# Forget sums of cached pages moved into the projection, and three small stages made one

## The chip, the cores and the metric

The kernel is one launch on 1 core of one Trainium2 chip. The metric is the device time of that launch in microseconds (us), lower is better. TensorE (PE) multiplies matrices, VectorE (DVE) and ScalarE (ACT) do elementwise work, GpSimd (POOL) helps with both and issues gathers, SyncE (SP) issues most transfers. "DMA queue" below is the row of transfers that one of these engines has issued; all of SP's go through the profile's queue q1.

## The reference: what is computed

One layer of a decoder over a prompt of 2,048 tokens (prefill) and over 8 requests of 8 new tokens, each with 8,192 cached positions in 64 pages of 128.

```python
p = einsum('btd,de->bte', x, w_in)          # q | k | v | 8 forget logits | 512 pooling channels
logf = log_sigmoid(f_logit + b_f)
qc = cumsum(logf, axis=1)                   # forget sums of the new tokens
kc_past = lf_past - cumsum(lf_past, axis=1, reverse=True)   # of the cached positions
s = q.k * ATTN_SCALE + qc[query] - kc[key]; p = softmax(causal(s)); att = p @ v
pool[g] = window_mean(u[g], 2**(g+1)) - u[g]; pool = (pool @ w_pool) * pool_scale
x1 = layer_norm(ALPHA * x + concat(att, pool) @ w_out)
x2 = layer_norm(ALPHA * x1 + conv_ffn(x1))
```

`kc_past` of a cached position is minus the sum of the forget terms of all later cached positions of its request. `cache_logf` holds one row per page: 128 positions x 8 heads, 4 KB; `page_table` says which pages a request owns.

## The kernel before

The work is a row of stages. Each is a block of its own with one instruction stream per engine; its end waits until its transfers have landed, clears its semaphores and passes a barrier of all engines. Every matrix product in fp32 is three products of rounded parts (`hi`, `lo`).

**`stage_project`** (tiles `A_`). `w_in` comes in eight 1 MB chunks through the two halves of `prow`; ACT makes `w_hi` (L289), DVE `w_lo` (L326), and only then may SP load the next chunk into that half (`w_lo_done`). Then 17 tiles of 128 tokens with 5 column groups each. PE does a group's 24 products (L214 to L216); ACT copies out groups 0, 2, 4 and DVE groups 1 and 3 (L313). Between groups PE turns q, k and u of the tile before (L226) and the next x (L198); DVE makes the rests of both (L318, L303). POOL copies the gates and splits v. SP stores the results and loads the x of a tile ahead (L151).

**`stage_gates_pool`** (tiles `B_`). SP loads eight constants and the 4 MB `uT`. DVE makes the log-sigmoid as a chain of short instructions, `lf`; PE sums it (`ps_s`, `ps_c`); DVE scales and splits the sums into `css` and `ch`. SP stores them (`negc_s`, `aug`). Then for each of four pooling groups DVE makes window sums and `pooled` (L488 to L496), PE multiplies with `w_pool` (L530), ACT scales (L510), SP stores `poolT` (L439, L441).

**`stage_prepare`** (tiles `E_`). It readies decode attention. SP loads constants, four copies of the sample queries, the keys and `negc_s`, and copies v into groups (`vgrp`, L1116). DVE clears `qbd` and `wn`, transposes q, k and `negc_s`, spreads q into the block-diagonal `qbd` (L1155), and SP stores it. PE makes the logits among new tokens, DVE adds a mask and keeps them (`snew`, L1161). Then four rounds, each for 128 pages (two requests): POOL gathers 128 rows of `cache_logf` (L1135); DVE sums each page (L1168) and makes `rest` (L1169); PE transposes `lin` (L1210), DVE copies (L1174), PE multiplies with triangular `later` and with ones (L1218, L1220), DVE scales (L1180) and transposes a 128x4096 tile (L1184), and SP stores 2 MB of `wT` (L1124).

**`stage_attention`** (tiles `C_`, prefill). DVE sets rows of `q2` and `k2` to one (L718, L719); these lie in `X_x_hi` and `X_x_lo`. Only then SP loads head 0 in eight transfers: six of 512 KB from `sc_qk` (each 64 partitions x 8 KB, L634) and two of 16 KB from `aug` (L635, L636), then its v (1 MB, L639), then head 1 the same way. PE's first logits (L657) wait for all eight transfers of head 0 and for two small identities (`C_both`, L624). Later heads are loaded when a buffer comes free.

**`stage_mix_prompt`, `stage_ffn_decode`, `stage_sample`** follow. `stage_ffn_decode` (tiles `F_`) runs the prompt's FFN with decode attention interleaved; per 8 pages it loads a bias tile `wT` (L1864) and adds it to the logits with one product per half, `sel` x `wT` (L1475).

Of the kernel before, what the change touches and what calls it, by code (L numbers as in the profile page):

```python
# [10 lines left out]
I32 = mybir.dt.int32  # L11
# [75 lines left out]
def stage_project(nc, io, sc, persist):  # L87
# [20 lines left out]
    with ExitStack() as ctx:  # L108
# [9 lines left out]
        stp = m.sb("stp", [P, PW])  # L118
        ps_x = m.ps("x", [P, 2, 512])
# [14 lines left out]

        block = ctx.enter_context(nc.Block())

        @block.sync
        def _(sp):
            sp.dma_start(ident[:, :], io["c_ident"]).then_inc(i_in, 16)
            sp.dma_start(xin[:, :], io["x_prompt"][0, 0:P, :]).then_inc(x_in, 16)  # L140
            for c in range(DC):
                if c >= 2:
                    sp.wait_ge(w_lo_done, c - 1)
                sp.dma_start(prow[:, c % 2, :], io["w_in"][0, c * P:(c + 1) * P, :]).then_inc(raw_in[c], 16)
# [11 lines left out]
            for t in range(TILES):  # L156
# [15 lines left out]
                if t + 2 < NT1:  # L172
                    load(t + 2)

# [13 lines left out]
            for done in (qk_stored, v_stored, u_stored):  # L188
                sp.wait_ge(done, 16 * TILES)

        @block.tensor
        def _(pe):
# [39 lines left out]
            for t in range(NT1):  # L232
                for g in range(NG):
# [3 lines left out]
                    if g == 2 and t + 1 < NT1:  # L237
                        x_transposes(t + 1)

# [60 lines left out]
        def _(dve):  # L300
# [21 lines left out]

            x_rest(0)
# [4 lines left out]
            for t in range(NT1):  # L328
                for g in range(NG):
# [4 lines left out]
                    if g == 2 and t + 1 < NT1:  # L334
                        x_rest(t + 1)
            dve.wait_ge(tail, 1)
# [9 lines left out]
        def _(pool):  # L346
            for t in range(TILES):
                evacuated(pool, NG * t + 4, p_act, p_dve)
# [24 lines left out]

def stage_gates_pool(nc, io, sc, persist):
    with ExitStack() as ctx:
        m = Mem(nc, ctx, "B")
        ident, fgate, uTs = persist["ident"], persist["fgate"], persist["uTs"]
# [19 lines left out]
        mixed = m.sb("mixed", [P, 2, SEQ + S])  # L397
        ps_c = m.ps("c", [P, 512])
# [12 lines left out]
        chain = m.sem("chain")  # L411

# [4 lines left out]
        def _(sp):  # L417
# [8 lines left out]
            sp.dma_start(uT[:, :, MAXW:], sc["uT"].rearrange("g p t -> p g t")).then_inc(u_in, 16)  # L426

# [5 lines left out]
            sp.dma_start(sc["negc_s"], css[:, :]).then_inc(stored, 16)  # L433
            sp.wait_ge(ch_ready, 4)
            for k in range(4):
                sp.dma_start(sc["aug"][:, k, :].rearrange("h (t p) -> t h p", p=P), ch[:, k, :]).then_inc(stored, 16)
# [5 lines left out]
            sp.wait_ge(stored, 16 * 7)  # L442
# [4 lines left out]
        def _(dve):  # L447
            link = Link(dve, chain)
            nc.vector.memset(ones[:, :], 1.0)
            nc.vector.memset(uT[:, :, 0:MAXW], 0.0)  # L450
            dve.wait_ge(consts, 16 * NCONST)
# [20 lines left out]
            for k in range(2):  # L472
                nc.vector.tensor_tensor(ch[:, 2 * k + 1, :].bitcast(F32R), cs[:, k, :], ch[:, 2 * k, :], ALU.subtract)\
                    .then_inc(ch_ready, 1)
            dve.wait_ge(u_in, 16)

            n = MAXW + SEQ
            for g in range(G):
# [5 lines left out]
                for k in range(g + 1):  # L484
# [13 lines left out]
                    0.5 ** (g + 1), uTs[:, g, :, MAXW - 1:], ALU.mult, ALU.subtract).then_inc(pooled_ready, 1)  # L498

# [15 lines left out]
        def _(pe):  # L515
# [7 lines left out]
            nc.tensor.matmul(ps_c[:, 0:P], before[:, :], tot[:, :], start=False, stop=True).then_inc(c_ready, 1)  # L523
            for g in range(G):
# [9 lines left out]

def stage_attention(nc, io, sc, persist):
# [55 lines left out]
    with ExitStack() as ctx:  # L594
        m = Mem(nc, ctx, "C")
        ident, causal, identb, att = persist["ident"], persist["causal"], persist["identb"], persist["att"]
        K2 = HD + 4
        qs, ks = m.sb("qs", [P, 2, SEQ], F32R), m.sb("ks", [P, 2, SEQ], F32R)
        q2, k2 = (persist[n][0:K2, :, :].rearrange("p c t -> p (c t)").rearrange("p (a s) -> p a s", a=2)
                  for n in ("x_hi", "x_lo"))  # L600
# [11 lines left out]
        head_in = [m.sem("head_in0"), m.sem("head_in1")]  # L612
        v_in = [m.sem("v_in0"), m.sem("v_in1")]
        c_in, ones_set = m.sem("c_in"), m.sem("ones_set")
# [8 lines left out]
        def _(sp):  # L623
            sp.dma_start(both[0:HD, :], io["c_ident"][0:HD, 0:HD]).then_inc(c_in, 16)  # L624
            sp.dma_start(both[HD:P, :], io["c_ident"][0:HD, 0:HD]).then_inc(c_in, 16)
            for h in range(H):
                par, c, rows = h % 2, h // 2, slice((h % 2) * HD, (h % 2 + 1) * HD)
                if h < 2:
                    sp.wait_ge(ones_set, 1)
                else:  # L630
                    sp.wait_ge(s_done, piece_of[4 * (h - 1), 0])
                for dst, a in ((qs[0:HD, par, :], 0), (qs[HD:P, par, :], 1), (ks[0:HD, par, :], 2),
                               (ks[HD:P, par, :], 2), (q2[0:HD, par, :], 0), (k2[0:HD, par, :], 3)):
# [1781 lines left out]
```

## Time and profile before

| | |
|---|---|
| time, median of 3 runs | 3626.79 us (3623.26 to 3629.71) |
| the profiled execution: its time | 3626.13 us |
| the profiled execution: its span | 3624.5 us |
| PE busy | 3187.7 us, 88% of the span |
| DVE busy | 2116.4 us, 58% |
| ACT busy | 1744.9 us, 48% |
| POOL busy | 671.6 us, 19% |
| granted TensorE clock, mean | 0.948 of full |

The span is the stretch that the profile covers; the device time of the same execution is 1.63 us longer. Busy shares are averages over stages. Since stages are separated by barriers, the time of the kernel is the sum of the stages' times, and each stage has its own limit: an engine, a chain of engines that wait for each other, or a queue of transfers.

### The profile page before, as it was taken

To read this page: it belongs to the slowest core of one execution; us is meant where nothing else is said; L and a number is where in the kernel's file an instruction comes from. 1 tells how busy PE (TensorE), PEld (TensorE's weight loads), DVE (VectorE), ACT (ScalarE), POOL (GpSimd) and SP (SyncE) were. 2 spreads that over 40 slices of the span, in tenths; PEclk is the share of its full clock that TensorE was granted. 3 is DMA by queue.
4 is the path that set the end of the run, shared out by engine and by line. 5 is a ranking of instruction groups with operands and counts; after the bars stand their busy time and mean duration, and the time that the engine had idled before them with its cause. 6 is when DMAs were issued, how large, how long until landed. Compare 5 with 4: busy or idle time off the path is not lost. (4 is left out here: it accounts for less than half of the span.)

```text
span 3624.5 us, 58231 instructions
## 1 busy us (share of the span) xinstructions
PE 3187.7 (88%) x20136; PEld 2520.7 (70%) x20136; DVE 2116.4 (58%) x3638; ACT 1744.9 (48%) x3493; POOL 671.6 (19%) x1194
## 2 busy tenths in 40 slices
PE   6999953488888897999989999999999899999858
PEld 5999941367777686777767777777777677777623
DVE  2111155477767554666677666677666776665655
ACT  2111110266666311456645666545666456666445
POOL 0000000000000011323323333233332233322100
PEclk9999976699999998999999999999999999999979
DMA  4333333423230335657777677787676776757575
GB/s 145 111 115 105 111 125 134 126 63 79 67 75 1 117 131 169 221 178 246 257 257 277 233 240 243 277 287 247 224 248 231 276 281 235 248 199 255 193 270 210
DMA packets 269003, 680.25 MB, mean 188 GB/s; under 512 B 40023, under 2 KB 119799, under 8 KB 259711
## 3 DMA queue, kind: packets, MB, share of 16 engines
q1 hardware_dynamic: 175911, 371.85, 31.5%
q0 software_dynamic: 88768, 290.00, 23.0%
q10 hardware_dynamic: 4032, 14.68, 1.1%
q8 instruction: 161, 2.64, 0.3%
q14 instruction: 131, 1.07, 0.1%
HBM read 599.23 MB, written 77.82 MB: 187 GB/s over the span
## 5 line engine op out<-in xcount | busy, mean ns | idle before, releaser
L1424 PE MATMUL F_ps_u<-X_x_hi,F_w_hi 128*128 128x512 f32 x1408 | 574.9, 408 | 6.5 <-DVE F_w_lo L1666 6.5
L1425 PE MATMUL F_ps_u<-X_x_lo,F_w_hi 128*128 128x512 f32 x1408 | 554.6, 394 | 0.0
L1426 PE MATMUL F_ps_u<-X_x_hi,F_w_lo 128*128 128x512 f32 x1408 | 553.9, 393 | 0.0
L1666 DVE TENSOR_TENSOR F_w_lo<-X_raw,F_w_hi 128x512 fp32r<-128x512 f32 x470 | 320.7, 686 | 383.3 <-ACT F_w_hi L1564 382.8
L1856 POOL DMA_DIRECT2D F_kin<-cache_k x512 | 276.8, 541 | 686.8 <-DVE F_kt L1720 497.2
L1564 ACT CAST F_w_hi<-X_raw 128x512 fp32r<-128x512 f32 x470 | 287.6, 615 | 223.7 <-PE F_ps_y L1426 98.4
L1720 DVE STREAM_TRANSPOSE F_kt<-F_kin 128x1024 f32<-128x1024 f32 x256 | 303.1, 1221 | 60.6 <-PE F_ps_t L1480 45.8
L1882 POOL DMA_DIRECT2D F_vin<-cache_v x512 | 281.9, 551 | 293.4 <-issue 170.6
L1424 PEld LDWEIGHTS F_ps_u<-X_x_hi,F_w_hi 128*128 128x128 f32 x1408 | 267.4, 190 | 97.9 <-issue 26.2
L1424 PE MATMUL F_ps_y<-F_w_hi,F_g_hi 128*128 128x512 f32 x704 | 294.7, 419 | 40.4 <-DVE F_w_lo L1666 40.3
L1426 PEld LDWEIGHTS F_ps_u<-X_x_hi,F_w_lo 128*128 128x128 f32 x1408 | 267.1, 190 | 58.2
L1425 PEld LDWEIGHTS F_ps_u<-X_x_lo,F_w_hi 128*128 128x128 f32 x1408 | 267.8, 190 | 48.8
L1425 PE MATMUL F_ps_y<-F_w_lo,F_g_hi 128*128 128x512 f32 x704 | 284.4, 404 | 0.0
L1426 PE MATMUL F_ps_y<-F_w_hi,F_g_lo 128*128 128x512 f32 x704 | 283.9, 403 | 0.0
L1666 DVE TENSOR_TENSOR F_w_lo<-F_raw,F_w_hi 128x512 fp32r<-128x512 f32 x234 | 160.0, 686 | 201.0 <-ACT F_w_hi L1564 200.8
L741 DVE TENSOR_TENSOR C_p_lo<-C_ps_t,C_p_hi 128x512 fp32r<-128x512 f32 (+1 forms) x320 | 192.7, 609 | 137.4 <-ACT C_p_hi L787 135.8
L214 PE MATMUL A_ps_p<-A_w_hi,A_x_hi 128*128 128x412 f32 (+1 forms) x680 | 243.9, 359 | 25.8 <-DVE A_w_lo L326 25.8
L778 ACT ACTIVATE C_row<-C_row,C_least 128x1024 f32<-128x1024 f32 (+2 forms) x192 | 173.1, 902 | 172.7 <-DVE C_row L729 140.2
L1588 ACT ACTIVATE F_h<-F_ps_u,F_coef 128x512 f32<-128x512 f32 x176 | 120.8, 686 | 248.6 <-PE F_ps_u L1426 248.6
L216 PE MATMUL A_ps_p<-A_w_hi,A_x_lo 128*128 128x412 f32 (+1 forms) x680 | 240.4, 354 | 0.0
L215 PE MATMUL A_ps_p<-A_w_lo,A_x_hi 128*128 128x412 f32 (+1 forms) x680 | 240.2, 353 | 0.0
L787 ACT CAST C_p_hi<-C_ps_t 128x512 fp32r<-128x512 f32 (+1 forms) x320 | 163.4, 517 | 132.8 <-PE C_ps_t L676 131.3
(296 smaller groups left out, 6289.1 us busy)
## 6 DMA issues: line engine op xcount, KB each, us to landing
F_kin<-cache_k POOLq DMA_DIRECT2D x512, 256.0 KB, 4.1
F_vin<-cache_v POOLq DMA_DIRECT2D x512, 256.0 KB, 4.5
X_raw<-w_up_t SPq DMA_DIRECT2D x118, 512.0 KB, 5.1
X_raw<-w_down SPq DMA_DIRECT2D x117, 512.0 KB, 5.3
F_raw<-w_down SPq DMA_DIRECT2D x59, 512.0 KB, 5.5
F_raw<-w_up_t SPq DMA_DIRECT2D x58, 512.0 KB, 5.1
S_raw<-w_up_t SPq DMA_DIRECT2D x22, 1024.0 KB, 10.4
sc_qk<-A_qk SPq DMA_DIRECT2D x16, 1024.0 KB, 5.7
```

Of the source, the lines that this page charges most:

```text
L214: nc.tensor.matmul(out, x_hi[:, t % 2, c, :], w_hi[:, c, cols], start=c == 0, stop=False)
L215: nc.tensor.matmul(out, x_hi[:, t % 2, c, :], w_lo[:, c, cols], start=False, stop=False)
L216: last = nc.tensor.matmul(out, x_lo[:, t % 2, c, :], w_hi[:, c, cols], start=False, stop=c == DC - 1)
L741: nc.vector.tensor_tensor(p_lo[:, i % PBUF, o:512], ps_t[:, tick_of[i] % 3, o:512], p_hi[:, i % PBUF, o:512].bitcast(F32), ALU.subtract).t ...
L1424: nc.tensor.matmul(out, a_hi, b_hi, start=first, stop=False)
L1425: nc.tensor.matmul(out, a_hi, b_lo, start=False, stop=False)
L1426: return nc.tensor.matmul(out, a_lo, b_hi, start=False, stop=last)
L1564: nc.scalar.copy(w_hi[:, q % 4, :], raw[unit % RAW][:, q % 2 * 512:(q % 2 + 1) * 512]).then_inc(hi_done, 1)
L1666: nc.vector.tensor_tensor(w_lo[:, q % 4, :], raw[q // 2 % RAW][:, q % 2 * 512:(q % 2 + 1) * 512], w_hi[:, q % 4, :].bitcast(F32), ALU.subt ...
L1720: nc.vector.transpose(kt[:, :, half % 2 * 64:(half % 2 + 1) * 64].rearrange("p f (j t) -> p j f t", j=2), kin[:, half % KR, :, :].rearrang ...
L1856: pool.dma_start(kin[:, half % KR, j, :], io["cache_k"][ds(pages[j], 1), :, :].rearrange("a t c -> (a t) c"))\
L1882: pool.dma_start(vin[j:P:4, n % 2, :, :], io["cache_v"][ds(pages[j], 1), :, :].rearrange("a (b t) c -> (a t) b c", b=4))\
```

## The change

1. `stage_prepare` is gone as a stage.
2. Forget terms of cached pages: the four gathers of `cache_logf` are issued by POOL during the projection, and DVE sums them there by doubling steps (`cached_forget`), one step in each slot after a column group. PE adds one product per 128 pages (`later_pages`). `wT` has another layout, 512 KB per 128 pages, and is stored by SP in the projection. Two small loads stand ahead of the weights in SP's queue.
3. Queries, keys, `snew`, `qbd` and `vgrp` are made in `stage_gates_pool`; `negc_s` isn't stored and loaded but copied from tile to tile (`ncs`). `qbd` and the ones are set by POOL. That stage also loads the first two heads of the prefill attention (`load_head`, `load_forget`).
4. `stage_attention` loads only v for heads 0 and 1.
5. `stage_mix_prompt` puts half of `w_lo` and its `e` tiles in the space of `ks` and `qs`; sizes and orders stay. `uTs`, `fgate`, `snew` and `attT_s` share one tile, `late`.
6. In `stage_ffn_decode` the bias tile has 32 rows in place of 128, and so has `sel`.

```diff
 stage_project, sync:
             sp.dma_start(xin[:, :], io["x_prompt"][0, 0:P, :]).then_inc(x_in, 16)
+            sp.dma_start(ids[:, :], io["page_rows"]).then_inc(pages_in, 16)
+            sp.dma_start(latep[:, :], io["c_latep"]).then_inc(pages_in, 16)
             for c in range(DC):
...
                 if t + 2 < NT1:
                     load(t + 2)
+                if t % SPAN == SPAN - 1:
+                    sp.wait_ge(w_ready, t // SPAN + 1)
+                    sp.dma_start(sc["wT"][t // SPAN].rearrange("r p k -> p r k"),
+                                 wout[:, :].rearrange("p (r k) -> p r k", k=32)).then_inc(w_stored, 16)
 stage_project, tensor:
+            def later_pages(i, t):
+                pe.wait_ge(l_summed, i + 1)
+                pe.wait_ge(hi_out, t)
+                pe.wait_ge(lo_out, t)
+                nc.tensor.matmul(ps_t[:, 0, 0:H], latep[:, :], lin[:, i % 2, 0:H], start=True, stop=True).then_inc(after_pe, 1)
             def qku_transposes(t):
                 evacuated(pe, NG * (t + 1), p_act, p_dve)
+                pe.wait_ge(after_read, (t + SPAN - 1) // SPAN)
...
+                    if g == 4 and t % SPAN == 1 and t < TILES:
+                        later_pages(t // SPAN, t)
 stage_project, vector, after each group (t, g):
+            def cached_forget(t, g):
+                i, k = t // SPAN, NG * (t % SPAN) + g
+                cur = lin[:, i % 2, :]
+                n = PAGE * H
+                if k < 7:
+                    d = H << k
+                    if k == 0:
+                        dve.wait_ge(l_in[i % 2], 16 * (i // 2 + 1))
+                    step = nc.vector.tensor_tensor(cur[:, 0:n - d], cur[:, 0:n - d], cur[:, d:n], ALU.add)
+                    if k < 6:
+                        link(step)
+                    else:
+                        step.then_inc(l_summed, 1)
+                if k == 9:
+                    dve.wait_ge(after_pe, i + 1)
+                    nc.vector.tensor_scalar(after[:, :], ps_t[:, 0, 0:H], 1.0 / SCALE, None, ALU.mult).then_inc(after_read, 1)
+                if k == 11:
+                    dve.wait_ge(after_read, i + 1)
+                    dve.wait_ge(l_summed, i + 1)
+                    if i:
+                        dve.wait_ge(w_stored, 16 * i)
+                    out = wout[:, :].rearrange("p (h t) -> p h t", h=H)
+                    nc.vector.tensor_copy(out[:, :, PAGE - 1], after[:, :])
+                    nc.vector.scalar_tensor_tensor(out[:, :, 0:PAGE - 1], cur.rearrange("p (t h) -> p h t", h=H)[:, :, 1:PAGE],
+                                                   1.0 / SCALE, after[:, :].unsqueeze(2).to_broadcast([P, H, PAGE - 1]),
+                                                   ALU.mult, ALU.add).then_inc(w_ready, 1)
 stage_project, gpsimd:
+            pool.wait_ge(pages_in, 32)
+            gather(0)
+            gather(1)
             for t in range(TILES):
+                if t in (SPAN, 2 * SPAN):
+                    gather(t // SPAN + 1)
 new functions:
+def load_head(sp, sc, persist, h):
...
+    for dst, a in ((qs[0:HD, par, :], 0), (qs[HD:P, par, :], 1), (ks[0:HD, par, :], 2),
+                   (ks[HD:P, par, :], 2), (q2[0:HD, par, :], 0), (k2[0:HD, par, :], 3)):
+        sp.dma_start(dst.bitcast(F32), sc["qk"][a, c, rows, :]).then_inc(head_in[par], 16)
+def load_forget(sp, sc, persist, h):
...
+    sp.dma_start(q2[HD:HD + 2, par, :].bitcast(F32), sc["aug"][h, 0:2, :]).then_inc(head_in[par], 16)
+    sp.dma_start(k2[HD + 2:HD + 4, par, :].bitcast(F32), sc["aug"][h, 2:4, :]).then_inc(head_in[par], 16)
 stage_gates_pool, sync:
             sp.dma_start(uT[:, :, MAXW:], sc["uT"].rearrange("g p t -> p g t")).then_inc(u_in, 16)
+            for b in range(4):
+                sp.dma_start(q4[b * 32:(b + 1) * 32, :, :], sc["q_s"].rearrange("(g r) c -> r g c", g=2)).then_inc(qin, 16)
+            sp.dma_start(ks[:, :, :], io["k_sample"].rearrange("(g r) c -> r g c", g=2)).then_inc(qin, 16)
+            for dst, name in ((sel[:, :, :], "c_seln"), (nmask[:, :], "c_nmask"), (rowmask[:, :], "c_rowmask")):
+                sp.dma_start(dst, io[name]).then_inc(cin, 16)
+            for h in range(2):
+                load_head(sp, sc, persist, h)
+            for s in range(NB):
+                sp.dma_start(sc["vgrp"][s], io["v_sample"][32 * (s // 4):32 * (s // 4) + 32, :]).then_inc(q_stored, 16)
             sp.wait_ge(lf_ready, 1)
...
             sp.wait_ge(cs_ready, 2)
-            sp.dma_start(sc["negc_s"], css[:, :]).then_inc(stored, 16)
+            sp.wait_ge(zero, 1)
+            for g in range(2):
+                sp.dma_start(ncs[:, g, 0:H], css[32 * g:32 * g + 32, :]).then_inc(ncs_in, 16)
...
+            sp.wait_ge(qbd_ready, 1)
+            sp.dma_start(sc["qbd"].rearrange("s p c -> p s c"), qbd[:, :, :, :, :].rearrange("p s f b q -> p s (f b q)"))\
+                .then_inc(q_stored, 16)
+            sp.wait_ge(aug_stored, 64)
+            sp.wait_ge(ones_set, 2)
+            for h in range(2):
+                load_forget(sp, sc, persist, h)
             for g in range(G):
                 sp.wait_ge(mixed_ready, g + 1)
 stage_gates_pool, vector, between the last split of ch and the pooling:
+            dve.wait_ge(qin, 80)
+            nc.vector.transpose(qT[:, :, :, :], q4[:, :, :].rearrange("p g (f t) -> p g f t", t=32)).then_inc(qT_ready, 1)
+            nc.vector.transpose(kT[:, :, :, :], ks[:, :, :].rearrange("p g (f t) -> p g f t", t=32))
+            dve.wait_ge(ncs_in, 32)
+            nc.vector.transpose(ncT[:, :, :], ncs[:, :, :]).then_inc(kT_ready, 1)
...
+            last.then_inc(qbd_ready, 1)
             dve.wait_ge(u_in, 16)
```

## Rows read from the trace of the kernel before

**Rows 1.** Windows by stage, columns in the first row.

```profile
core 0: us, PE busy (x) PEld busy (x) DVE busy (x) ACT busy (x) POOL busy (x), PEclk, DMA share, GB/s
...
46.00:480.00 434.00, 418.38 (x2337) 410.74 (x2335) 60.14 (x82) 66.60 (x115) 32.70 (x49) 1.00 0.34 105
...
487.96:557.98 70.02, 25.90 (x48) 12.00 (x48) 44.83 (x67) 10.82 (x21) 0.00 (x0) 0.62 0.42 133
557.98:654.95 96.97, 32.58 (x140) 17.45 (x140) 57.40 (x51) 0.00 (x0) 3.99 (x4) 0.62 0.38 144
654.95:681.90 26.95, 0.00 (x0) 0.00 (x0) 6.94 (x2) 0.00 (x0) 0.00 (x0) 0.50 0.64 148
```

**Rows 2.** Waits, 480 to 700 us: total us, times, longest.

```profile
PE C_ps_s L657 <- DMA X_x_lo<-sc_aug: 40.7, 1, 40.7
```

**Rows 3.** Timeline of SP's queue: start, us taken to issue, line, transfer.

```profile
492.04 0.43 SPq L426 DMA_DIRECT2D B_uT<-sc_uT  x1
...
502.68 1.54 SPq L431 DMA_DIRECT2D logf_sample<-B_lf  x1
...
560.74 1.84 SPq L1113 DMA_DIRECT2D E_q<-sc_q_s  x4
...
563.09 5.00 SPq L1116 DMA_DIRECT2D sc_vgrp<-v_sample  x8
568.14 0.57 SPq L1118 DMA_DIRECT2D E_ncs<-sc_negc_s  x1
...
654.95 0.55 SPq L624 DMA_DIRECT2D C_both<-c_ident  x1
...
663.64 1.09 SPq L634 DMA_DIRECT2D C_qs<-sc_qk  x2
...
667.83 0.26 SPq L636 DMA_DIRECT2D X_x_lo<-sc_aug  x1
```

**Rows 4.** DMA issues, 488 to 560 us: count, KB each, us to landing.

```profile
B_uT<-sc_uT SPq DMA_DIRECT2D x1, 4096.0 KB, 12.4
sc_poolT<-B_mixed SPq DMA_DIRECT2D x4, 1024.0 KB, 5.0
...
sc_negc_s<-B_css SPq DMA_DIRECT2D x1, 2.0 KB, 1.6
```

**Rows 5.** Windows of four us, columns as in the first group.

```profile
496.00:500.00 4.00, 0.00 (x0) 0.00 (x0) 3.59 (x13) 0.00 (x0) 0.00 (x0) 0.50 1.00 426
...
668.00:672.00 4.00, 0.00 (x0) 0.00 (x0) 0.00 (x0) 0.00 (x0) 0.00 (x0) 0.50 1.02 217
```

**Rows 6.** Timeline of VectorE, 506 to 577 us.

```profile
506.41 2.30 DVE L488 TENSOR_TENSOR B_wa<-B_uT 128x2063 f32<-128x2063 f32 x1
...
542.47 0.22 DVE L496 SCALAR_TENSOR_TENSOR B_pooled<-B_sb,AB_uTs 128x64 f32<-128x64 f32 x1
...
573.54 3.02 DVE L1155 COPY E_qbd<-E_qT 32x512 f32<-32x512 f32 x8
```

**Rows 7.** Tile of the projection's raw weights, 0 to 45 us.

```profile
L289 ACT CAST A_w_hi<-A_prow x8: 1904/1905/1907, 10.2 to 40.5; 128x2056 fp32r<-128x2056 f32 x8
...
DMA to landing us min/median/max: 4.7/5.0/5.6
```

**Rows 8.** Tile of the gathered forget terms; us to landing.

```profile
L1135 POOL DMA_INDIRECT E_lin<-cache_logf,E_ids x4: 932/950/1158, 562.4 to 600.6; - x4
...
DMA to landing us min/median/max: 5.0/5.6/6.2
```

**Rows 9.** Groups, 557 to 655 us: busy us, mean ns, idle before.

```profile
L1210 PE MATMUL E_ps_l<-all_ident,E_lin 128*128 128x128 f32 x32 | 5.1, 312 | 0.0
```

**Rows 10.** Timeline of VectorE within one prompt tile of the projection.

```profile
76.84 0.59 DVE L313 COPY A_prow<-A_ps_p 128x412 f32<-128x412 f32 x1 [1.61 <-PE A_ps_p L216]
84.53 1.23 DVE L303 TENSOR_TENSOR A_x_lo<-A_ps_x,A_x_hi 128x1024 fp32r<-128x1024 f32 x1 [7.11 <-ACT A_x_hi L267]
```

**Rows 11.** Waits, 46 to 480 us: total us, times, longest.

```profile
PE A_ps_x L198 <- DMA A_xin<-x_prompt: 14.6, 14, 1.9
```

More of the change, by code:

```diff
@@ L133, in stage_project @@
         tail, tail_copied, st_done = m.sem("tail"), m.sem("tail_copied"), m.sem("st_done")
+        pages_in, chain = m.sem("pages_in"), m.sem("chain")
+        l_in = [m.sem("l_in0"), m.sem("l_in1")]
+        l_summed, after_pe, after_read, w_ready, w_stored = (
+            m.sem(n) for n in ("l_summed", "after_pe", "after_read", "w_ready", "w_stored"))
+        SPAN = 4
         block = ctx.enter_context(nc.Block())
@@ L397, in stage_gates_pool @@
         mixed = m.sb("mixed", [P, 2, SEQ + S])
+        q4 = m.sb("q4", [P, 2, AW])
+        qT = m.sb("qT", [P, 2, 16, 32])
+        qbd = m.sb("qbd", [P, NB, 16, 4, NT])
+        ks = m.sb("ks", [32, 2, AW])
+        kT = m.sb("kT", [32, 2, 16, 32])
+        ncs, ncT = m.sb("ncs", [32, 2, 32]), m.sb("ncT", [32, 2, 32])
+        sel = m.sb("sel", [32, 2, P])
+        nmask, rowmask = m.sb("nmask", [P, 32], BF16), m.sb("rowmask", [P, NB])
+        ps_n = m.ps("n", [P, 2, 2, 32])
         ps_c = m.ps("c", [P, 512])
@@ L450, in _ @@
             nc.vector.memset(uT[:, :, 0:MAXW], 0.0)
+            nc.vector.memset(ncs[:, :, :], 0.0).then_inc(zero, 1)
             dve.wait_ge(consts, 16 * NCONST)
@@ L474, in _ @@
                     .then_inc(ch_ready, 1)
+            dve.wait_ge(qin, 80)
[3 more added lines that the diff above has]
+            nc.vector.transpose(ncT[:, :, :], ncs[:, :, :]).then_inc(kT_ready, 1)
+            dve.wait_ge(qT_ready, 1)
+            dve.wait_ge(qbd_zero, 1)
+            for b in range(4):
+                for g in range(2):
+                    part = slice(b * 32, (b + 1) * 32)
+                    last = nc.vector.tensor_copy(
+                        qbd[part, 4 * g:4 * g + 4, :, b, :].rearrange("p s f q -> p f s q"),
+                        qT[part, g, :, :].rearrange("p f (s q) -> p f s q", s=4))
+            last.then_inc(qbd_ready, 1)
             dve.wait_ge(u_in, 16)
@@ L498, in _ @@
                     0.5 ** (g + 1), uTs[:, g, :, MAXW - 1:], ALU.mult, ALU.subtract).then_inc(pooled_ready, 1)
+            dve.wait_ge(cin, 48)
+            dve.wait_ge(n_done, 1)
+            dve.wait_ge(pooled_ready, G)
+            for s in range(NB):
+                nc.vector.tensor_scalar(persist["snew"][:, s, :, :], ps_n[:, s // 4, :, :], rowmask[:, s:s + 1], None, ALU.add)
         @block.scalar
@@ L523, in _ @@
             nc.tensor.matmul(ps_c[:, 0:P], before[:, :], tot[:, :], start=False, stop=True).then_inc(c_ready, 1)
+            pe.wait_ge(cin, 48)
+            pe.wait_ge(qT_ready, 1)
+            pe.wait_ge(kT_ready, 1)
+            for g in range(2):
+                for st in range(2):
+                    out = ps_n[:, g, st, :]
+                    nc.tensor.matmul(out, sel[:, st, :], ncT[:, g, :], start=True, stop=False, skip_group_check=True)
+                    nc.tensor.matmul(out, identb[:, :], nmask[:, :], start=False, stop=False, skip_group_check=True)
+                    for half in range(2):
+                        for hs in range(4):
+                            f = 2 * (4 * st + hs) + half
+                            last = nc.tensor.matmul(out[32 * hs:32 * hs + 32, :], qT[0:32, g, f, :], kT[:, g, f, :],
+                                                    start=False, stop=half == 1, skip_group_check=True)
+            last.then_inc(n_done, 1)
             for g in range(G):
@@ L2313, in constants @@
     st_o, hs_o, q_o = r // 64, r // 8 % 4, r % 8
-    c["c_sel"] = np.stack([(r[:, None] // 32 == b[None, :]) & (r[:, None] % 32 == 4 * st + hs[None, :])
+    row = np.arange(32)
+    c["c_sel"] = np.stack([(row[:, None] % 4 == b[None, :]) & (row[:, None] // 4 == 4 * st + hs[None, :])
                            for st in range(2)], 1).astype(f)
```

249 lines of the change are left out of this document (62 added, 187 removed).

## The prediction

> **What bounds the kernel now.** I read the windows by stage first, because barriers between stages make the time a sum of stages [rows 1]. In the projection PE is busy 418 of 434 us, so PE is the limit there. The three stretches behind it are different: PE is busy 26 of 70.0 us in the gates and pooling, 33 of 97.0 us in the preparation of decode, and 0 of 27.0 us between the start of the attention stage and its first logits. None of this lies beside other work, so what leaves these 194 us leaves the time one for one.
>
> Then the waits: PE waits 40.7 us, until 681.9, for a 16 KB transfer of forget sums [rows 2]. The timeline of SP's queue explains it: the transfer is issued at 667.83, and lands 14 us later, where another small one lands in 1.6 [rows 3, 4]. Ahead of it in the queue stand six transfers of 512 KB issued from 663.64 on. So in this trace a small transfer on SP's queue lands when the bulk ahead of it is through. I come back to that, since the change puts small transfers behind more bulk.
>
> **What is removed.** The whole preparation stage, 96.97 us [rows 1]: its barrier, its constants, four rounds and its last store. Its work on q, k and `snew` comes back in the stage before (below). At the start of attention the ones no longer hold the loads up, and the six big transfers of heads 0 and 1 are already in. PE then waits only for the two identities: the first is issued as the stage begins, in 0.55 us [rows 3], the second takes as long, and lands about 1.6 us after its issue [rows 4]. I take 2.7 us from stage start to first logits, in place of 26.95, a gain of 24.25. The v of head 0 (1 MB) is issued right behind the identities; a 1 MB store lands in 5.0 us [rows 4], so it is there some 6 us into the stage, after which the exponentials and turns of the first group still have to run. If logits had to wait for it, that costs 3.5 us; I keep that for the range.
>
> **What is added to the gates and pooling stage.** All of SP's new transfers stand ahead of the two little copies `ncs`, and VectorE waits for `ncs_in` before it spreads q and before it pools. Queued behind that wait on VectorE are the eight copies to `qbd`, then the whole pooling, for which PE, ACT and SP's stores of `poolT` wait in turn. So the question is when `ncs` lands.
> - `uT` is issued at 492.04 and lands after 12.4 us, at 504.4 [rows 3, 4].
> - Four copies of q, the keys and three constants are some 0.7 MB. Between the rates of 426 and 217 GB/s [rows 5] that is 1.6 to 3.2 us; I take 2.2.
> - Twelve transfers of 524,288 bytes to 64 partitions each are 6.29 MB. The same transfers run at 217 GB/s with all 16 DMA engines busy [rows 5], which makes 29.0 us.
> - Eight copies for `vgrp`, 0.52 MB: 2.0 us (1.2 to 5.0, the upper end being their issue time [rows 3]).
> - The two stores of `lf`, whose second took 1.54 us to issue, being held by the queue [rows 3]: 1.5 us.
> - The two `ncs` copies: 0.57 us each to issue, as the load that they replace [rows 3], and 1.6 to land [rows 4]: 2.7 us.
>
> The sum is 504.4 + 2.2 + 29.0 + 2.0 + 1.5 + 2.7 = 541.8. SP's own issuing is not the limit: the q copies take 1.84 us, `vgrp` 5.00 [rows 3], and twelve head transfers at half of 1.09 us each [rows 3] some 7, so SP is through at about 510. With the small transpose and the copies to `qbd` (3.02 us [rows 6]) pooling begins at 545.1, where it began at 506.41 [rows 6]: 38.7 us later. Everything behind it, 36.3 us of pooling on VectorE to 542.7 [rows 6] and 15.3 us until the stage ends [rows 1], moves along unchanged. Bounds: 33 (0.7 MB, `vgrp` and `lf` at their lowest and part of it already done when `uT` lands) to 46 (all at their highest, and 200 GB/s for the heads).
>
> The rest is covered. The transposes of q and k run while VectorE waits. PE's logits among new tokens run before the first `pooled` is ready. `snew` comes after the last `pooled`, in the 15.3 us in which PE, ACT and SP finish. The store of `qbd`, the `aug` stores and the four small loads of `aug` stand behind `ncs` on SP, and the first `mixed` is ready more than 10 us after `ncs`. POOL's fills of `qbd`, `q2` and `k2` are not in this trace: VectorE waits until 541.8 for something else, so they cost nothing as long as the first takes under 53 us from 488; without that cover it would be its own duration.
>
> **What is added to the projection.** At the start two small transfers go ahead of the weights: 2 x 0.43 us of issue, the length of `uT`'s [rows 3], 0.9 us. Two gathers of 512 KB then share the DMA engines with the first weight chunks: at 426 GB/s up to 2.5 us. Each chunk lands in 5.0 us and ACT works 1.9 on it [rows 7], after which VectorE frees the buffer and the chunk after next may go; so a delay of the first pair passes on to the last, and PE with it. The gathers are issued about 1 us each by POOL and land in 5.6 [rows 8], when part of the first pair is in. I take 1.8; together 2.7 (0.9 to 5.0).
>
> PE gets four products 128x8. The nearest row is 0.31 us for 128x128 [rows 9]; with its own weight load I take 0.4 each, 1.6 us in all (0.4 to 2.5).
>
> VectorE's steps: 7 per round over 6,152 elements; 2,063 took 2.30 us [rows 6], so 6.9 us, and about 1.3 for the last. Four rounds are 33 us, in slots of at most 1.3. VectorE idles 1.61 and 7.11 us before its evacuation and the rest of x [rows 10], so they are hidden; uncovered they would cost the 33 us. VectorE's wait for `after_pe` falls where its next work comes a group later. The `wT` store is 4,096 runs of 128 bytes; 2,048 runs of 512 land in 5.0 us [rows 4], so 10 us. It is issued behind the load of x, and the next load of x comes one tile later (434 us by 17 is 25.5), so it is covered too; PE does wait for x in each tile, 14.6 us in all [rows 11], so anything that came before x would be paid in full. The gathers 2 and 3 run when SP's queue is nearly empty. The smaller decode bias tile and the shared tiles of the later stages I count as nothing: products keep their columns.
>
> **Sum.** -96.97 - 24.25 + 38.7 + 2.7 + 1.6 = -78.2 us. The profiled execution took 3626.13 us (span 3624.5), 0.66 below the median. That gives 3547.9 on its scale and 3548.6 on the median's; I forecast 3548. With all bounds on one side the sum is -87 or -64, so this case runs from 3539 to 3563.
>
> **Rivals.**
> - *`ncs` does not wait for the heads.* Then SP's issuing decides: `ncs` is issued at 511 and lands at 513.4, pooling starts at 516.8, 10.4 us late, and the time is 3520. Against it stands the small transfer that took 14 us behind bulk [rows 2, 3]. The Trainium skill, DMA: Bandwidth & Descriptors, section Queues, rings and completion order, says that completion is not first-in-first-out per issuing engine, though each DMA engine takes its descriptors in order. By the first half of that rule the time would be this rival's; the trace shows the second. Chance 0.08.
> - *The head loads run at the 426 GB/s of `uT`.* 14.8 in place of 29.0 us: 3534. Against it: the very same transfers at 217 with the DMA engines full [rows 5]. The Trainium skill, SBUF — State Buffer, section Door 1: The DMA port swizzle, has it that 64 neighbouring partitions reach half of the ports; the trace agrees, 217 of 426. Chance 0.05.
> - *The projection pays.* Its forget work gets in front of x, by a slow `wT` store or a late VectorE, and PE's waits for x double: some 15 us and more with what follows each, 3564. Chance 0.10.
> - *Slower than before.* The `wT` store jams SP's queue. Four stores must each cost 19.5 us on top of 25.5 us of cover, so each would have to last 45 us where I reckon 10; from there on the change loses, and at 50 us each it pays 4 x 24.5 = 98 us against 78.2, which is 3647. For it speaks only that no transfer of 128-byte runs of this size is in the trace. Chance 0.02.
>
> My own case has 0.75. The range reaches from the second rival to the third: 3531 to 3566; outside are the first and last, and a little more. A difference under 0.2% (7 us) is about what a measurement of this kernel can't tell from no change. Every case but the last is faster by far more: faster 0.97, same 0.01, slower 0.02.
>
> **What would show it.** A wait of VectorE of 30 us or more for `ncs`, ending near 542 plus the projection's delay, and a pooling that runs as before from there on; first logits under 4 us after attention begins; a projection longer by 4 us, nearly all of it in its first 50. If `ncs` lands within 5 us of its issue, or PE waits more for x than now, the prediction is wrong there.

## The result, and the profile after

The changed kernel takes 3571.27 us (median of 4 runs, 3569.3 to 3574.85), the kernel before on the same chip 3627.76 (4 runs, 3623.26 to 3629.71). The ratio is 0.9846, 95% interval 0.9834 to 0.9859: 56.5 us less, where 78.2 were forecast, and 5 us above the range. The profiled execution has a span of 3567.9 us against 3624.5.

**Up to the first logits** the forecast nearly holds: 82.3 us are gained there, where it had 78.2 in all. Windows by stage of the kernel after, columns as in [rows 1]: the end of the projection, the joint stage, and attention up to its first logits.

```profile
46.00:482.00 436.00, 419.10 (x2347) 411.55 (x2347) 99.04 (x123) 66.65 (x115) 40.41 (x51) 1.00 0.40 112
490.03:596.99 106.96, 30.85 (x124) 15.94 (x124) 55.25 (x87) 10.84 (x21) 10.52 (x3) 0.58 0.65 178
596.99:599.60 2.61, 0.02 (x1) 0.02 (x1) 0.00 (x0) 0.00 (x0) 0.00 (x0) 0.50 0.24 38
```

The preparation stage's 96.97 us are gone, the stage of gates and pooling has grown from 70.02 to 106.96, and attention waits 2.61 us for its first logits in place of 26.95 [rows 1]. The first logits come at 599.6 against 681.9: 82.3 us earlier. What makes the joint stage long stands in SP's queue (timeline: start, us taken to issue), in the landing times (DMA issues, 488 to 560 us), in the waits, and in VectorE's timeline:

```profile
499.68 2.42 SPq L446 DMA_DIRECT2D H_ks<-sc_qk  x2
...
512.58 0.58 SPq L532 DMA_DIRECT2D logf_prompt<-B_lf  x1
513.20 26.77 SPq L533 DMA_DIRECT2D logf_sample<-B_lf  x1
540.08 1.20 SPq L537 DMA_DIRECT2D B_ncs<-B_css  x2
```

```profile
logf_prompt<-B_lf SPq DMA_DIRECT2D x1, 64.0 KB, 29.0
```

```profile
DVE B_ncT L592 <- DMA B_ncs<-B_css: 28.3, 1, 28.3
```

```profile
510.80 0.15 DVE L580 TENSOR_SCALAR B_css<-B_ps_s 64x8 f32<-64x8 f32 x1
...
542.43 0.23 DVE L592 STREAM_TRANSPOSE B_ncT<-B_ncs 32x64 f32<-32x64 f32 x1 [28.28 <-DMA B_ncs<-B_css]
542.60 3.02 DVE L598 COPY B_qbd<-B_qT 32x512 f32<-32x512 f32 x8
545.64 2.31 DVE L615 TENSOR_TENSOR B_wa<-B_uT 128x2063 f32<-128x2063 f32 x1
```

The sums for `ncs` are there at 510.8, but a 2 KB store in front of their copies takes 26.77 us to issue, since the heads' loads and the copies of v stand ahead of it (with these moved behind, in a run below, the same store takes 1.32 us). The copies are issued at 540.08, `ncs` lands at 542.4 (541.8 forecast, without the projection's delay), pooling starts at 545.6 (545.1), and everything behind it is as before.

**The loss is in the decode**, some 750 us further on, in the stage that runs the prompt's feed-forward with decode attention between its products. From the first `w_hi` x `x_hi` product of the feed-forward's `u` to the start of the last `w_hi` x `g_hi` product of its `y`, in the kernel before and then in the one after:

```profile
1435.80:3436.70 2000.90, 1914.18 (x13406) 1473.06 (x13407) 1317.75 (x2122) 1165.87 (x2362) 609.62 (x1118) 0.98 0.72 244
1353.90:3376.80 2022.90, 1941.99 (x13405) 1467.31 (x13406) 1320.62 (x2122) 1167.34 (x2362) 611.44 (x1118) 0.98 0.70 239
```

That is 22.0 us more. The 82 us ahead at its start are 60 at its end. Its product for the cached bias is the only one whose shape changed. Groups of the kernel before and then of the one after (busy us, mean ns | idle before, and what ended it):

```profile
L1475 PE MATMUL F_ps_t<-F_wT,F_sel 128*128 128x128 f32 x512 | 113.1, 303 | 20.8 <-DMA F_wT<-sc_wT 9.9 <-DVE F_kt L1720 9.1 <-DVE F_pt L1726 1.8
L1475 PEld LDWEIGHTS F_ps_t<-F_wT,F_sel 128*128 128x128 f32 x512 | 85.7, 189 | 60.1 <-issue 39.1 <-DVE F_kt L1720 11.7
```

```profile
L1460 PE MATMUL F_ps_t<-F_wT,F_sel 32*128 32x128 f32 x512 | 124.9, 324 | 19.6 <-DMA F_wT<-sc_wT 9.5 <-DVE F_kt L1705 8.2 <-DVE F_pt L1711 1.9
L1460 PEld LDWEIGHTS F_ps_t<-F_wT,F_sel 32*128 32x128 f32 x512 | 75.7, 184 | 91.6 <-issue 81.0 <-DVE F_kt L1705 10.6
```

These are single fp32 products and not three of rounded parts, and so are those with the keys and values; the profile records each in two parts (x512 for 256 bias products). A quarter of the rows, yet the products are no shorter, and the weight loads sit idle 91.6 us before them in place of 60.1, mostly for "issue": no semaphore holds them. Where it goes is seen in the timeline of TensorE within one decode unit, before and then after. The first number is the start; the durations overlap, so read the distances between starts.

```profile
2003.02 0.39 PE L1426 MATMUL F_ps_u<-X_x_hi,F_w_lo 128*128 128x512 f32 x1
2003.25 0.38 PE L1475 MATMUL F_ps_t<-F_wT,F_sel 128*128 128x128 f32 x2
2003.56 0.64 PE L1480 MATMUL F_ps_t<-F_kt,F_qbd 128*32 128x128 f32 x16
2004.14 0.49 PE L1475 MATMUL F_ps_t<-F_wT,F_sel 128*128 128x128 f32 x2
2004.56 0.65 PE L1480 MATMUL F_ps_t<-F_kt,F_qbd 128*32 128x128 f32 x16
2005.02 1.05 PE L1491 MATMUL F_ps_d<-F_vin,F_pt 128*32 128x256 f32 x16
2005.99 0.50 PE L1424 MATMUL F_ps_u<-X_x_hi,F_w_hi 128*128 128x512 f32 x1
```

```profile
1930.78 0.39 PE L1411 MATMUL F_ps_u<-X_x_hi,F_w_lo 128*128 128x512 f32 x1
1931.10 0.48 PE L1460 MATMUL F_ps_t<-F_wT,F_sel 32*128 32x128 f32 x2
1931.51 0.64 PE L1465 MATMUL F_ps_t<-F_kt,F_qbd 128*32 128x128 f32 x16
1932.09 0.48 PE L1460 MATMUL F_ps_t<-F_wT,F_sel 32*128 32x128 f32 x2
1932.50 0.64 PE L1465 MATMUL F_ps_t<-F_kt,F_qbd 128*32 128x128 f32 x16
1932.96 1.05 PE L1476 MATMUL F_ps_d<-F_vin,F_pt 128*32 128x256 f32 x16
1933.94 0.50 PE L1409 MATMUL F_ps_u<-X_x_hi,F_w_hi 128*128 128x512 f32 x1
```

From the last feed-forward product to the bias product 0.23 became 0.32, from there to the products with the keys 0.31 became 0.41; the rest is equal. That is 0.19 us in each of 128 units (one unit is the decode work on four pages between two feed-forward products), 24 us. A shape is written rows*columns of the weights: 128*128 for the feed-forward, 128*32 for the products with keys and values, 32*128 for the new bias product. Only the first of the two bias products of a unit pays: the second stands between 128*32 products, and before the change too it was 0.42 from its successor. Going from the feed-forward's rounded products to an fp32 product of the same shape costs nothing: 0.23 before the change, as between two feed-forward products.

### The profile page after: what moved, and what is told of

It is laid out like the page before. It is cut to its first block and busy times, and to the rows that moved or that the text cites. A ratio compares the mean times of both kernels' runs of the same rounds, so it can differ in the third digit from the quotient of the medians.

```text
span 3567.9 us, 58096 instructions
## 1 busy us (share of the span) xinstructions
PE 3188.2 (89%) x20080; PEld 2501.6 (70%) x20080; DVE 2104.7 (59%) x3645; ACT 1747.0 (49%) x3493; POOL 689.7 (19%) x1197
## 5 line engine op out<-in xcount | busy, mean ns | idle before, releaser
L818 PE MATMUL C_ps_t<-all_ident,C_row 128*128 128x128 f32 x1088 | 179.9, 282 | 43.1 <-ACT C_row L917 42.1
```

## The experiments

Twelve kernels in three groups ran, each group beside the kernel before on its chip (3628.72, 3631.18 and 3628.75 us). All ratios are to that. Differences in us between kernels of two groups are differences of medians from two chips, on which the kernel before differed by up to 3.4 us.

**Rows of the bias product.** First the changed kernel with 128 rows again:

```diff
-        wT = m.sb("wT", [32, 2, 2 * P]); sel = m.sb("sel", [32, 2, P])
+        wT = m.sb("wT", [128, 2, 2 * P]); sel = m.sb("sel", [128, 2, P])   # rows 32 to 127 set to 0 once
-    row = np.arange(32)
+    row = np.arange(128)
```

> The changed kernel, with the bias product of decode attention over all 128 rows again (rows 32 to 127 of both operands hold zeros; the load stays 32 rows). Theory A, the narrow product: with 32 rows a unit of decode attention takes 0.19 us longer on TensorE (2.84 against 2.65 us to 2.74 from the first bias product on, and 0.09 before it), 128 units are 24 us. Then this kernel takes 3547 us, its FFN stage is 22 us shorter than that of the changed kernel, and weight loads ahead of the bias product wait some 40 us in all and not 81. Theory B: the FFN stage is longer because of the clock that this execution was granted or of what the stages before left behind. Then it takes 3571 us.

Measured: 3550.36 us, ratio 0.9777 (0.9756 to 0.9798), 21 less than the changed kernel (25 by the ratios). Its distances in a unit are those of the kernel before, and the decode runs 2004.5 us. The reverse, on the kernel before:

```diff
-    nc.tensor.matmul(out, sel[:, st, :], wT[:, n // 2 % 2, ...
+    nc.tensor.matmul(out, sel[0:32, st, :], wT[0:32, n // 2 % 2, ...
```

> The kernel before, with only the first 32 rows of the bias product used (it leaves out the bias of three of four new-token rows; loads and everything else stay). Theory A: the narrow product alone costs its 22 to 24 us, 3651 us. Theory B, clock or stages before: no change, 3627 us. Theory C, the 32-row loads are what slows the stage: no change either, since the loads stay as they were.

Measured: 3649.49 us, ratio 1.0057 (1.004 to 1.0074), 20.8 more, with 2022.3 us of decode. So the shape of this product alone takes about 21 us in either kernel. Whether it goes by the number of rows, a run with 64 tells (the first edit with 64 in place of 128):

> The changed kernel with 64 rows in the bias product of the decode (selection and bias tile of 64 rows, rows 32 to 63 zero). Theory (TensorE pays for leaving and entering its products over all 128 rows, whatever the smaller number is): as with 32 rows, 3571. Rival (the cost belongs to 32 rows alone, or grows as the rows fall): 3550 as with 128 rows, or halfway, 3560.

Measured: 3569.63 us, ratio 0.9828 (0.9811 to 0.9844): as 32 rows.

**Per change of shape, or per product?** Both bias products of a unit go first, then all 16 products with the keys:

```diff
     for st in range(2):
-        out = ...; nc.tensor.matmul(out, sel[:, st, :], wT[...], start=True, stop=False)
-        for half in range(2): ...          # 8 products with the keys
+        nc.tensor.matmul(ps_s[:, st * P:(st + 1) * P], sel[:, st, :], wT[...], start=True, stop=False)
+    for st in range(2):
+        for half in range(2): ...
```

> The changed kernel, 32 rows kept, with both bias products of a decode unit issued one behind the other ahead of the 16 products with the keys; before, bias, 8 products, bias, 8 products. Theory (the loss is paid at each change between 32-row and 128-row products): four changes a unit become two, so half of the 21 us comes back, about -10, plus whatever the same reordering gives at 128 rows. Rival (the loss is in each 32-row product itself): only what the reordering gives at 128 rows.

> The same reordering on the kernel with 128 rows (3550): both bias products first, then the 16 products with the keys. If going between products of all 128 columns and those of 32 columns costs nothing, 3550. If each such change costs the 0.09 to 0.15 us by which the starts in the trace are further apart than the work between them, two fewer in each of 128 units give -20 to -30: 3520 to 3530.

Measured: 3538.13 us with 32 rows, ratio 0.9748 (0.9732 to 0.9764), and 3516.13 with 128, ratio 0.9686 (0.967 to 0.9702). In both, the start flag of the second product drops the bias that the first one left for its rows. The reordering gives 33 and 34 us, 32 rows in place of 128 still cost 22. By my count of "four changes made two" the 32-row kernel should have gained 10 more than the other; it did not, and here the theory as I had put it fell. The count was wrong: the products with the keys are of another shape too, 128*32. With them the unit goes through 5 changes after, 4 before, 3 with 32 rows together and 2 with 128 rows together. The timeline of the last:

```profile
1908.47 0.39 PE L1412 MATMUL F_ps_u<-X_x_hi,F_w_lo 128*128 128x512 f32 x1
1908.70 0.61 PE L1462 MATMUL F_ps_t<-F_wT,F_sel 128*128 128x128 f32 x4
1909.24 1.08 PE L1470 MATMUL F_ps_t<-F_kt,F_qbd 128*32 128x128 f32 x32
1910.13 1.05 PE L1481 MATMUL F_ps_d<-F_vin,F_pt 128*32 128x256 f32 x16
1911.11 0.50 PE L1410 MATMUL F_ps_u<-X_x_hi,F_w_hi 128*128 128x512 f32 x1
```

To hold "per product" against "per change" once more, every bias product was issued twice in a row, which adds products and no change (`matmul(...)` doubled, the second overwriting the first):

> The changed kernel with every bias product of 32 rows issued twice (the second overwrites the first with the same values; 256 products more, no change of shape more). Theory (each change of a product's shape costs TensorE 0.13 to 0.17 us; the products themselves cost the same at any number of rows): by the 0.23 us by which four recorded parts in place of two put the next product off, 59 us more: 3630, which is the same step as the run with 128 rows makes. Rival (each 32-row product costs 0.08 to 0.1 us more than a 128-row one, because its weights are not loaded ahead): 20 to 26 us more than that, 3650 to 3656.

> The same doubling on the kernel with 128 rows (3550): 256 products more at 0.23 us are 59 us, 3609. With the run of 32 rows beside it, the difference of the two is what 32 rows cost: 21 as before if the cost is per change of shape, 41 to 47 if it is per product.

Measured: 3628.91 us with 32 rows, ratio 0.9997 (0.9986 to 1.0008), and 3597.09 with 128, ratio 0.9915 (0.99 to 0.993). They are 32 us apart, where the single products were 21; per product it would have been 42. The doubled 128-row kernel is 47 us above the single one, 12 less than the 59 expected, the 32-row one 58. So the times alone lie between the two theories. The granted clock accounts for the gap. Over the decode it was 0.983 with 128 rows doubled and 0.975 with 128 single, 0.973 and 0.975 with 32 rows. An estimate, from the clock records of these traces: I take (1 - granted clock) x duration as lost to the lower clock (1.2 in place of 2.4 GHz) and subtract it from each decode.

```
decode in us             duration  lost  rest
128 rows, single           2004.5  49.3  1955.2
128 rows, doubled          2047.6  35.5  2012.1
32 rows, single            2022.9  50.3  1972.6
32 rows, doubled           2086.4  56.4  2029.9
```

Doubling then costs 57 us in both, and the rows 17 to 18 us in both, not twice as much in the second. Over the six traces with 32 or 64 rows and this order of products the rest is 1972.6 to 1976.2, over the three with 128 it is 1955.2 to 1957.3: some 19 us apart. (Of the 22.0 us between the first two profiles, 6 are lower clock by this estimate, and 16 are left.) In the timeline of the doubled 32-row kernel one sees each distance by itself:

```profile
1899.04 0.40 PE L1411 MATMUL F_ps_y<-F_w_hi,F_g_lo 128*128 128x512 f32 x1
1899.36 0.48 PE L1460 MATMUL F_ps_t<-F_wT,F_sel 32*128 32x128 f32 x2
1899.69 0.38 PE L1462 MATMUL F_ps_t<-F_wT,F_sel 32*128 32x128 f32 x2
1900.00 0.64 PE L1467 MATMUL F_ps_t<-F_kt,F_qbd 128*32 128x128 f32 x16
```

The product after a change is followed 0.33 us later and the one ahead of the next change 0.31, where two like neighbours of 128 rows are 0.22 apart. So a change costs about 0.09 us ahead of it and 0.10 behind. The medians over the 103 to 107 units of each kernel in which no row waits for a semaphore, from the last feed-forward product ahead of a unit to the first behind it (worked out from the starts in the timelines):

```
kernel                             changes  distances in us                           sum
before; after with 128 rows           4     0.23 0.31 0.57 0.42 0.46 0.98             2.97
after; before with 32; with 64        5     0.32 0.41 0.57 0.41 0.46 0.98             3.16
together, 32 rows                     3     0.32 0.64 0.90 0.98                       2.83
together, 128 rows                    2     0.23 0.54 0.90 0.98                       2.64
twice, 32 rows                        5     0.32 0.32 0.31 0.57 0.32 0.31 0.46 0.98   3.60
twice, 128 rows                       4     0.23 0.22 0.32 0.57 0.33 0.32 0.46 0.98   3.42
```

32 rows in place of 128 cost 0.18 or 0.19 in every pair, once a unit, however many products have them; two changes less save 0.33; a product more of either kind costs 0.22. Times 128 that would be 24 us for the rows and 42 for the reordering, where 21 and 33 to 34 were measured. The traces suggest why: summed in the same way over all 128 units, the kernel before has 400.9 us and the one after 422.6; of these 21.7 us the 107 units without a wait bring 20.2, and the 21 in which TensorE waits anyway only 1.5, where two traces with the same products differ by 4.0.

**The queue ahead of `ncs`.** The copies go over ScalarE's queue:

```diff
-            for g in range(2):
-                sp.dma_start(ncs[:, g, 0:H], css[32 * g:32 * g + 32, :]).then_inc(ncs_in, 16)
...
             nc.scalar.activation(ex[:, :], mag[:, :], ACT.Exp, scale=-1.0).then_inc(ex_ready, 1)
+            act.wait_ge(zero, 1); act.wait_ge(cs_ready, 2)
+            for g in range(2):
+                act.dma_start(ncs[:, g, 0:H], css[32 * g:32 * g + 32, :]).then_inc(ncs_in, 16)
```

> The changed kernel, with the two small copies of the negated sums issued by ScalarE on its own queue and not by SP. Theory, queue order: VectorE's wait of 28 us for them was the bulk of the head loads ahead of them on SP's queue. On another queue they land 2 to 4 us after their issue at 511, pooling starts at 517 to 519 and not at 545.6, and the kernel takes 3543 us (28 us less). Rival: the 16 DMA engines are busy with the head loads whichever queue it is, and the copies wait as long as before: 3571 us. Second rival: they pass, but the store of the block-diagonal queries and the forget sums stay behind the heads until 541 and the stage ends no sooner than some 565, which is still before the pooling ends: no cost.

> Both edits together: bias product over 128 rows, small copies on ScalarE's queue. If the two causes are independent, the gains add: 3571 - 24 - 28 = 3519 us. If the queue edit only moves the wait to the loads of the first heads, 3547.

Measured: 3550.38 us, ratio 0.9783 (0.9766 to 0.98), and with 128 rows 3530.61, ratio 0.9726 (0.9709 to 0.9743): 21 and 41 less than the changed kernel, so the two causes add up. In time, they are 7 and 12 us short of what I expected. Timelines of ScalarE's queue and of VectorE with the copies on ScalarE:

```profile
512.67 1.47 ACTq L636 DMA_DIRECT2D B_ncs<-B_css  x2
```

```profile
523.53 0.23 DVE L589 STREAM_TRANSPOSE B_ncT<-B_ncs 32x64 f32<-32x64 f32 x1 [7.75 <-DMA B_ncs<-B_css]
```

On a queue of their own, two copies of 1 KB still land some 10 us after their issue, beside the heads' loads. The other way is to leave the queue and take the heads out of the front: their loads, and the copies of v, go behind the stores of `aug`.

```diff
-            for h in range(2):
-                load_head(sp, sc, persist, h)
-            for s in range(NB): ...                     # copies of v
             sp.wait_ge(lf_ready, 1)
...
             for k in range(4):
                 sp.dma_start(sc["aug"][:, k, :]...).then_inc(aug_stored, 16)
+            for h in range(2):
+                load_head(sp, sc, persist, h)
+            for s in range(NB): ...
```

> The changed kernel, with the loads of the first two heads and the copies of v moved behind the stores of aug on the same SP queue; nothing else moves. Theory (the small copies into ncs are late because they are queued behind 6.29 MB on SP): with nothing ahead of them they land about 3 us after the sums are on VectorE (510.80), so pooling starts at about 518 in place of 545.6, the first logits at about 572, and the median falls by 27 less the 2.5 that the attention stage gave back when ncs went over ScalarE's queue: about 3546. Rival one (what delays ncs is that the 16 engines are busy, whatever the queue, as the 523.5 of the run with ncs on ScalarE would have it): nothing is in flight here, so it must fall to the same 518 too; if ncs still takes 11 us, its 32-byte pieces are the cost, and the time is that of that run, 3550. Rival two (the heads, now issued after 515, come too late for the attention stage): the first logits wait for H_ks, and the time is above 3550.

Measured: 3549.72 us, ratio 0.9773 (0.9757 to 0.9789). DMA issues of this kernel, then its SP queue and VectorE:

```profile
B_ncs<-B_css SPq DMA_DIRECT2D x2, 1.0 KB, 1.7
```

```profile
512.66 1.24 SPq L533 DMA_DIRECT2D B_ncs<-B_css  x2
...
529.99 13.76 SPq L451 DMA_DIRECT2D X_x_hi<-sc_aug  x1
...
545.42 10.28 SPq L552 DMA_DIRECT2D sc_poolT<-B_mixed  x1
```

```profile
518.94 2.31 DVE L615 TENSOR_TENSOR B_wa<-B_uT 128x2063 f32<-128x2063 f32 x1
```

The 2 KB store ahead of `ncs` now takes 1.32 us to issue, `ncs` lands in 1.7 us and pooling starts at 518.9 against 545.6, 26.7 us earlier, as expected. The first logits come only 21.5 earlier (578.1): SP's queue jams later, at the small loads of `aug` and the stores of `poolT`, and ScalarE, whose `mixed` buffers those stores hold, waits 20.1 us for them. The wait has moved and shrunk.

**The forget sums in the projection.** Six of the seven doubling steps of each round are taken out:

> The changed kernel without six of the seven doubling steps with which VectorE sums the cached forget terms in each round of the projection, so the sums are left out and the forget terms are wrong in value. Theory (VectorE's steps lie beside TensorE's projection and cost nothing; the 2.0 us by which the projection ends later come from the two small loads ahead of the first inputs and from the 32 gathers): 3571, no change. Rival (the steps hold up the projection through the casts and copies that share VectorE): up to 2 us less, at most 3569, which this measurement tells from no change only just; in the trace the store of k_sample, issued at 482.24, would come before 481.

Measured: 3568.49 us, ratio 0.984 (0.9825 to 0.9855) against 0.9846 with them: 2.8 us less, which the intervals don't tell from no change. The store of `k_sample`, by which I wanted to see the projection's end, came at 483.3 and not before 481, against 482.2 with the steps and 480.2 before. In other runs with the same projection it came between 481.2 (128 rows) and 487.2 (the version at the end), so a single trace can't show 2 us there. VectorE's steps are hidden, to within some 3 us.

**A version of its own**, from what the runs gave: 128 rows, bias products together with the second start flag off (`start=st == 0`), which keeps both biases, copies of v late, and the heads loaded by ScalarE's queue once `ncs` is in:

> A version of its own, from what the runs so far gave: 128 rows in the bias product; both bias products of a unit first, the second with its start flag off (with it on, the second product drops what the first one left, so that half of the rows lose their bias); v copies behind the stores of aug; and the loads of the first two heads on ScalarE's queue, after ncs has landed. Three parts are additive if they do not meet: 3516 of the reordered 128-row kernel, less the 21 that moving the heads gave, is 3495; the loads on a queue of their own should also free SP's stores of the pooled values (held 13.8 and 10.3 us with the heads ahead of them on SP), so that the first logits come before 578, at about 570: 3487. Rival: the heads, whatever the queue, take the engines that the pooled values' stores need; then the first logits stay at 578 and the time at 3495.

Measured: 3489.07 us (5 runs, 3485.62 to 3492.8), ratio 0.9615 (0.9602 to 0.9628): 140 us less than before, 82 less than the change by itself. From the start of the joint stage to the first logits it takes 82.6 us (494.9 to 577.5), the kernel with late heads 86.4 (491.7 to 578.1) and the changed one 109.6. Of the 8 us that I hoped for, 4 came: a store of the pooled values is still held 18.05 us in SP's queue.

## Why the prediction was off

By its own steps, in the traces:

- *The preparation stage goes, -96.97.* Right: nothing of it came back outside the projection and the joint stage.
- *First logits 2.7 us after attention begins.* Right: 2.61.
- *Pooling 38.7 us later.* Right in size, and in that `ncs` waits for the bulk ahead of it: 39.2 later, of which 2.1 are the later stage start, so 37.1; VectorE's wait was 28.3 us, not the 30 or more that was to be the sign. Wrong was "SP is through at about 510". SP stood at its 2 KB store until 540, so `ncs` wasn't waiting in the queue but was not issued yet. Both pictures end when the heads' loads are through, and so the sum came out. The rival by which `ncs` doesn't wait for the heads (3520) fell, and so did the one with heads at 426 GB/s: they ran at some 215. Behind bulk on SP the copies waited; only with nothing ahead did they land in 1.7 us.
- *Projection, 4.3 us.* The profiled pair shows 2.1, within what single traces of the same projection scatter. That VectorE's forget sums are hidden was right (no difference told without six of seven steps). The slower rival, the store of `wT` that jams SP, did not happen: the four stores landed in 8.4 us each, where 10 were reckoned, and PE's waits for x are 15.8 us in place of 14.6.
- *"The smaller decode bias tile and the shared tiles of the later stages I count as nothing: products keep their columns."* This is the step that failed. Columns kept, the product had the same 0.22 us; but with 32 rows it is of another shape than its 128*128 neighbour in front, and that made one change of shape more in each of 128 decode units, 0.19 us each. Taken out it gave back 21, put into the kernel before it cost 20.8. With 21 in the sum in place of nothing it would have been -57, which is 3569, where 3571 was measured. That it fits so closely is partly luck: up to the first logits the forecast was 4.1 us too small a gain (2.2 in the projection, 1.8 behind it), and 3.7 us of scatter outside the decode took that back.

The Trainium skill has a sentence on it that I did not weigh: TensorEngine Tiling (Array Packing), Key Properties, says that changing the tiling mode drains TensorE. The traces agree in that each change of shape cost 0.17 to 0.19 us, with 64 rows as with 32; that a drain is what costs it, no run here shows.

The rest of the difference between the first logits (-82.3) and the end (-56.6) is +0.4 up to the decode and +3.3 behind it, within the scatter of traces. The attention code is the same in all of them, and from first to last logits it took 514.8 us (before) to 524.4 (bias products together, 32 rows). Windows of these two:

```profile
681.90:1196.70 514.80, 445.08 (x2702) 363.60 (x2702) 368.86 (x835) 341.12 (x726) 0.00 (x0) 0.96 0.24 59
600.70:1125.10 524.40, 455.48 (x2703) 372.60 (x2704) 369.86 (x835) 341.71 (x726) 0.00 (x0) 0.94 0.22 53
```

The granted clock goes with it, here 0.965 and 0.944 (the third number from the end of each row, with a digit more): over all fourteen traces the stretch is longer nearly in the order in which time at the lower clock adds up, 18 to 29 us lost in the estimate used above. What stays open is why one execution is granted less than another, and how the 0.17 to 0.19 us of a change come about inside TensorE.

## What to carry to other kernels

Before shrinking the rows of a product to what its data needs, look at the shapes of its neighbours in TensorE's order: a product of a different shape costs a change going in or coming out, and zero rows that keep the shape are free; group products of one shape. And before putting bulk loads into a stage early, list the small transfers behind them on that queue for which somebody waits: here freeing two 1 KB copies from the 6.29 MB ahead of them was worth 21 us, and after that the next store in the queue became the wait.

## What I had not expected of the hardware

- A change between 128*128 and either 32*128 or 128*32, or between those two, costs TensorE 0.17 to 0.19 us in these units, split 0.09 ahead and 0.10 behind, and nothing in a wait table names it: it shows as "issue" of the weight load and in the distances between starts.
- A 2 KB store held SP 26.77 us at its issue, 1.32 us with no bulk ahead. No semaphore is waited for; the queue behind it stands still.
- POOL's fills slow VectorE. Timelines of VectorE and POOL in the changed kernel:

```profile
496.36 0.84 DVE L568 TENSOR_SCALAR B_mag<-all_late 128x136 f32<-128x136 f32 x1
497.23 0.30 DVE L569 TENSOR_TENSOR B_mag<-B_mag,all_late 128x136 f32<-128x136 f32 x1
497.91 2.85 DVE L430 TENSOR_SCALAR B_lp<-B_ex 128x136 f32<-128x136 f32 x1 [0.38 <-ACT B_ex L635]
```

```profile
493.60 3.50 POOL L684 MEMSET X_x_hi<- 4x4096 f32 x1
497.16 3.50 POOL L686 MEMSET X_x_lo<- 4x4096 f32 x1
```

  Both operations of kind TENSOR_SCALAR took 0.23 us before the change. Here the first ends at 497.20, as the first fill does at 497.10, and the second at 500.76, as the second fill does at 500.66. In the changed kernel the 2.6 us of the second are hidden by the wait for `ncs`; with the heads late they are on the path. The Trainium skill, SBUF — State Buffer, Who interferes with whom, has it that VectorE and GpSimd share a port pair under an exclusive lock, that `tensor_scalar` is among the operations that can contend for it, and that one with two SBUF inputs contends with a GpSimd instruction that reads SBUF, not with one that only writes it. The trace agrees: a fill only writes, and the two-input operation between the two kept its 0.30 while the second fill ran.
